# RWKV scan: whole transposes of the operands and of the inverse's levels, and direction 1 of A in the other half

## The reference

```python
def step(S, inp):
    rt, wt, kt, vt, at, bt = inp
    sa = jnp.einsum('bhvk,bhk->bhv', S, at)
    S = S * wt[:, :, None, :] + sa[..., None] * bt[:, :, None, :] + vt[..., None] * kt[:, :, None, :]
    return S, jnp.einsum('bhvk,bhk->bhv', S, rt)
```

## Time and profile before

| | |
|---|---|
| median of 3 runs | 2064.91 us (2064.57 to 2065.87) |
| profiled execution | 2068.68 us, span 2066.9 us |
| PE, PEld busy | 1737.8 us (84%), 1360.4 us (66%) |
| VectorE, ScalarE, GpSimd busy | 1111.6, 845.5, 288.4 us |
| the scan, 644 to 1113 us | PE 417.96 (x14716), PEld 403.63 (x14708), DVE 165.42, ACT 157.36, POOL 141.55 us busy |
| the stage ahead, 60 to 400 us | PE 340.00 us of 340 busy |
| mean granted TensorE clock | 0.929 of 2.4 GHz |

### The profile page before, as it was taken

The page is one execution under the profiler, slowest core; times in us unless marked ns, Lnnn a source line. Parts: engine busy times, 40 slices in busy tenths (PEclk is TensorE's granted clock), DMA queues, the critical chain, the costliest instruction groups (busy, mean ns, idle before and its releaser), DMA issues. The chain is left out here.

```text
span 2066.9 us, 47853 instructions
## 1 busy us (share of the span) xinstructions
PE 1737.8 (84%) x20423; PEld 1360.4 (66%) x20423; DVE 1111.6 (54%) x1786; ACT 845.5 (41%) x1228; POOL 288.4 (14%) x371
## 2 busy tenths in 40 slices
PE   5999999869896998989885698059999999999980
PEld 4777777757655888888885477046666666666650
DVE  4568898456753333333335632446565565656546
ACT  4256665212222333333332221046566565655632
POOL 0010000011103223332233000220000000000003
PEclk8999999989997999999997798579999999999995
DMA  5124454241102111111312121639998998999837
GB/s 170 62 93 136 137 147 123 66 158 62 61 1 91 49 55 55 55 30 54 145 65 84 54 73 50 247 132 378 362 381 348 372 371 350 377 363 379 350 143 254
DMA packets 95706, 355.62 MB, mean 172 GB/s; under 512 B 8984, under 2 KB 52295, under 8 KB 80936
## 3 DMA queue, kind: packets, MB, share of 16 engines
q1 hardware_dynamic: 82344, 306.83, 39.8%
q0 software_dynamic: 8576, 29.37, 3.7%
q10 hardware_dynamic: 4608, 16.78, 2.0%
HBM read 294.72 MB, written 56.13 MB: 170 GB/s over the span
## 5 line engine op out<-in xcount | busy, mean ns | idle before, releaser
L2236 DVE TENSOR_TENSOR e_rl<-proj,e_rh 128x1024 fp32r<-128x1024 f32 x256 | 304.9, 1222 | 150.1 <-ACT e_rh L2177 148.8
L2177 ACT ACTIVATE e_rh<-proj 128x1024 fp32r<-128x1024 f32 x256 | 258.6, 1053 | 82.4 <-PEq L1884 50.5
L51 PE MATMUL e_ph<-e_rh,e_xh 128*128 128x512 f32 x512 | 221.5, 433 | 17.1 <-DVE e_rl L2236 14.5
L2163 PE MATMUL e_py<-mix,proj 128*128 128x512 f32 x512 | 225.0, 592 | 0.7 <-issue 0.7
L51 PE MATMUL e_ph<-e_rh,e_xl 128*128 128x512 f32 x512 | 201.8, 394 | 0.0
L51 PE MATMUL e_ph<-e_rl,e_xh 128*128 128x512 f32 x512 | 200.5, 392 | 0.0
L51 PE MATMUL a_b<-a_xh,a_wh 128*128 128x512 f32 x432 | 177.9, 412 | 5.9 <-DVE a_wl L580 3.4
L51 PE MATMUL a_b<-a_xl,a_wh 128*128 128x512 f32 x432 | 170.2, 394 | 0.0
L51 PE MATMUL a_b<-a_xh,a_wl 128*128 128x512 f32 x432 | 170.2, 394 | 0.0
L2163 PEld LDWEIGHTS e_py<-mix,proj 128*128 128x128 f32 x512 | 97.1, 190 | 110.5 <-issue 108.1
L1544 ACT ACTIVATE s_th<-s_thb 128x512 f32<-128x512 f32 x128 | 76.4, 597 | 188.4 <-PE s_thb L1413 188.4
(11 more groups left out here) (352 smaller groups left out, 3260.1 us busy)
## 6 DMA issues: line engine op xcount, KB each, us to landing
proj<-in_moe_w SPq DMA_DIRECT2D x64, 2048.0 KB, 14.5
mix<-in_moe_w SPq DMA_DIRECT2D x32, 2048.0 KB, 8.7
proj<-scan_operands SPq DMA_DIRECT2D x64, 320.0 KB, 4.1
scan_operands<-late SPq DMA_DIRECT2D x64, 256.0 KB, 2.6
expert_rows<-e_yo ACTq DMA_DIRECT2D x32, 512.0 KB, 11.2
proj<-in_w_in SPq DMA_DIRECT2D x27, 512.0 KB, 4.1
proj<-in_x SPq DMA_DIRECT2D x16, 512.0 KB, 6.2
expert_rows<-proj SPq DMA_DIRECT2D x1, 7680.0 KB, 24.8
```

The lines of the kernel that those rows point to most:

```text
L51: m = e.matmul(out, lhs[a], rhs[b], start=first and n == 0, stop=last and n == 2)
L2163: m = e.matmul(py[h][:, :], at[:, k, :], w2[j][:, k, h * HALF:(h + 1) * HALF], start=(k == 0), stop=(k == KF - 1))
L2177: e.activation(rh[s % RING][:, :], piece(j, s), ACT.Copy).then_inc(high, 1)
L2236: e.tensor_tensor(rl[s % RING][:, :], piece(j, s), rh[s % RING][:, :].bitcast(F32), ALU.subtract).then_inc(low, 1)
```

## The change

`turn` no longer transposes quarter by quarter: eight whole 128 x 128 transposes for each g turn A, K, V and B. A whole transpose exchanges chunk and head halves together, and its result for direction 0 lies in one bank and for direction 1 in another; ScalarE copies the first, VectorE the second.

In the inverse, levels 2 to 5 no longer make both H and T by matmuls. Only T is made (at the last level H); a whole transpose of T, two for each g, gives H, and ScalarE copies it (`hu`) once VectorE has added the identity to the level's products. The products of levels 2 to 5 go to all four quarters: the half that the result is written to changes between chunk and unit. Results that come from different row halves of the array go to different banks of PSUM. Level 1 stays on the diagonal. The level's results of one g now share a pair of banks, so level 1 waits for VectorE's copy of the last inverse (`hf_kept`).

For direction 1, A is stored with its two chunks exchanged, by two DMAs in place of one (`a_out` counts 48 a unit instead of 32), so that `products` can write the B-A product into the other half; it has 20 matmuls for each g instead of 16. `a_k_v` and `inverse_applied` then also use all four quarters. A constant `eyes`, four identities, replaces the broadcast one in L1472.

The diff, without renamings of the same kind:

```diff
@@ -197,7 +197,13 @@
                         store(u, d, OP_R, ep2[d], r_out)
                     for d in range(2):
                         e.wait_ge(ra_done, 2 * u + d + 1)
-                        store(u, d, OP_A, ea2[d], a_out)
+                        if d == 0:
+                            store(u, d, OP_A, ea2[d], a_out)
+                        else:
+                            p, at = span(u)
+                            for c in range(2):
+                                e.dma_start(S.ops[p, d, at // P:at // P + 4, :, OP_A, (1 - c) * CH:(2 - c) * CH].rearrange("t p c -> p t c"),
+                                            ea2[d].rearrange("p (t k c) -> p t k c", k=2, c=CH)[:, :, c, :]).then_inc(a_out, 16)
                         e.wait_ge(b_done, 2 * u + d + 1)
                         store(u, d, OP_B, a2[d], b_out)
...
-        th, xx = sb("s_th", [P, GP, HU, 2, CH]), sb("s_xx", [P, GP, HU, CH])
+        tt, xx = sb("s_tt", [P, GP, HU, CH]), sb("s_xx", [P, GP, 2, 2, CH])
+        hu = sb("s_hu", [P, GP, 2, 2 * CH])
-        pu = sb("s_pu", [P, GP, HU, 2 * CH])
+        pu = sb("s_pu", [P, 2, HU, 2 * CH])
...
-        xb = [ps(f"s_x{k}", [P, HALF]) for k in range(GP)]
-        thb = [ps(f"s_thb{k}", [P, HALF]) for k in range(GP)]
-        w = [ps(f"s_w{k}", [P, HALF]) for k in range(4)]
-        xs = [t[:, 0:HU * CH].rearrange("p (u c) -> p u c", u=HU) for t in xb]
-        ths = [t.rearrange("p (u q c) -> p u q c", u=HU, q=2) for t in thb]
+        lv = [ps(f"s_lv{k}", [P, 2, HALF]) for k in range(GP)]
+        wb = [ps(f"s_w{k}", [P, 2, HALF]) for k in range(2)]
+        w = [wb[k][:, j, :] for k in range(2) for j in range(2)]
+        bank = [t.rearrange("p (q c) -> p q c", q=4) for t in (*(lv[k][:, j, :] for k in range(GP) for j in range(2)), *w)]
+        xs = [t[:, :, 0:2 * CH].rearrange("p b (q c) -> p b q c", q=2) for t in lv]
+        ts = [t[:, :, 2 * CH:4 * CH].rearrange("p b (q c) -> p b q c", q=2) for t in lv]
+        hus = [t[:, 0, 4 * CH:8 * CH].rearrange("p (q c) -> p q c", q=2) for t in lv]
-        trb = [t.rearrange("p (d s c) -> p d s c", d=2, s=4) for t in w[2:4]]
-        akvb = w[2].rearrange("p (u c) -> p u c", u=2 * HU)
+        trb = [t.rearrange("p (s c) -> p s c", s=4) for t in w[2:4]]
+        akvb = wb[1][:, :, 0:HU * CH].rearrange("p d (u c) -> p d u c", u=HU)
...
                         for u, (h, d) in enumerate(units):
-                            for c in hs:
-                                i = mm(pub[g][c, u, :], hf[c, g, u, :], rec[j][c, g, h, d, 0:2 * CH], start=True, stop=True)
-                        i.then_inc(pu_full, 1)
+                            for c in range(2):
+                                r = hs[c ^ d]
+                                i = mm(pub[d][hs[c], 2 * g + h, :], hf[r, g, u, :], rec[j][r, g, h, d, 0:2 * CH], start=True, stop=True)
+                            if g == GP - 1 and h == 1:
+                                i.then_inc(pu_full, 1)
 
                 def outputs_by_v(m):
 
...
-                    for d in range(2):
-                        for k, s in ((0, OP_B), (1, OP_K)):
-                            for h, c in quarters:
-                                i = mm(gb[h][hs[c], d, k, :], op[j][hs[h], g, d, s, hs[c]],
-                                       op[j][hs[h], g, d, OP_R:OP_A + 1, hs[c]], start=True, stop=True)
+                    for k, s in ((0, OP_B), (1, OP_K)):
+                        for h, c in quarters:
+                            mm(gb[h][hs[c], 0, k, :], op[j][hs[h], g, 0, s, hs[c]],
+                               op[j][hs[h], g, 0, OP_R:OP_A + 1, hs[c]], start=True, stop=True)
+
+                    ra = op[j][:, g, 1, OP_R:OP_A + 1, :].rearrange("p s (c t) -> p (s c) t", c=2)
+                    for h, c in quarters:
+                        mm(gb[h][hs[c], 1, 1, :], op[j][hs[h], g, 1, OP_K, hs[c]],
+                           ra[hs[h], 0:4:3, :] if c == 0 else ra[hs[h], 1:3, :], start=True, stop=True)
+                    for h, c in quarters:
+                        mm(gb[h][hs[c], 1, 0, 0:CH], op[j][hs[h], g, 1, OP_B, hs[c]], ra[hs[h], c, :], start=True, stop=True)
+                    for h, c in quarters:
+                        i = mm(gb[h][hs[1 - c], 1, 0, CH:2 * CH], op[j][hs[h], g, 1, OP_B, hs[c]], ra[hs[h], 3 - c, :],
+                               start=True, stop=True)
                     i.then_inc(g_full, 1)
 
                 def turn(f, g, back):
 
                     j = f % 2
                     if g == 1:
-                        e.wait_ge(tm_kept, f * 2 + 1)
+                        e.wait_ge(tm_kept, f * 4 + 2)
                     elif back is not None:
                         e.wait_ge(y_kept, back + 1)
                     for d in range(2):
                         for s in range(OP_A, N_OP):
-                            for h, c in quarters:
-                                i = mm(trb[h][hs[c], d, s - OP_A, :], op[j][hs[h], g, d, s, hs[c]], S.ident[hs[h], hs[h]],
-                                       start=True, stop=True)
+                            i = e.transpose(trb[d][:, s - OP_A, :], op[j][:, g, d, s, :], S.ident[:, :])
                     i.then_inc(turned, 1)
 
                 def a_k_v(f):
                     j = f % 2
-                    e.wait_ge(tm_kept, f * 2 + 2)
+                    e.wait_ge(tm_kept, f * 4 + 4)
                     e.wait_ge(g_kept, f * 2 + 2)
                     for g in range(GP):
-                        for u, (h, d) in enumerate(units):
-                            for c in hs:
-                                i = mm(akvb[c, g * HU + u, :], slot(j, g, h, d, S_KA)[c, :], slot(j, g, h, d, S_V)[c, :],
-                                       start=True, stop=True)
+                        for h, d in units:
+                            for c in range(2):
+                                i = mm(akvb[hs[c ^ d], d, 2 * g + h, :], slot(j, g, h, d, S_KA)[hs[c], :],
+                                       slot(j, g, h, d, S_V)[hs[c], :], start=True, stop=True)
                     i.then_inc(akv_full, 1)
 
...
                         fill[9] = lambda: a_k_v(front)
+                    pairs = [(q, p) for q in range(2) for p in range(2)]
                     e.wait_ge(t1_kept, n + 1)
                     for l in range(1, LEVELS):
                         first, last = l == 1, l == LEVELS - 1
@@ -1396,21 +1421,31 @@
                         for g in range(GP):
                             if not first:
                                 e.wait_ge(th_kept, n * 8 + (2 * (l - 2) + g + 1))
-                            for u in range(HU):
-                                for c in hs:
-                                    i = mm(xs[g][c, u, :], al[c, l - 1, g * HU + u, :],
-                                           t1[c, g * HU + u, :] if first else th[c, g, u, 0, :], start=True, stop=True)
+                            elif n:
+                                e.wait_ge(hf_kept, (n - 1) * 2 + (g + 1))
+                            for q, p in pairs:
+                                u = 2 * q + p
+                                for c in range(2):
+                                    to = xs[g][hs[c], p, q, :] if first else xs[g][hs[p], c, q, :]
+                                    i = mm(to, al[hs[c], l - 1, g * HU + u, :],
+                                           t1[hs[c], g * HU + u, :] if first else tt[hs[c], g, u, :], start=True, stop=True)
+                            if not first:
+                                for q in range(2):
+                                    i = e.transpose(hus[g][:, q, :], tt[:, g, 2 * q:2 * q + 2, :].rearrange("p u c -> p (u c)"),
+                                                    S.ident[:, :])
                             i.then_inc(x_full, 1)
                         fill[2 * l - 2]()
                         for g in range(GP):
                             e.wait_ge(x_kept, n * 10 + (2 * (l - 1) + g + 1))
-                            for u in range(HU):
-                                h0 = lambda c: h1[c, g * HU + u, :] if first else th[c, g, u, 1, :]
-                                if not last:
-                                    for c in hs:
-                                        mm(ths[g][c, u, 0, :], h0(c), xx[c, g, u, :], start=True, stop=True)
-                                for c in hs:
-                                    i = mm(ths[g][c, u, 1, :], xx[c, g, u, :], h0(c), start=True, stop=True)
+                            if not first:
+                                e.wait_ge(hu_kept, n * 8 + (2 * (l - 2) + g + 1))
+                            for q, p in pairs:
+                                u = 2 * q + p
+                                for c in range(2):
+                                    h0 = h1[hs[c], g * HU + u, :] if first else hu[hs[p], g, q, c * CH:(c + 1) * CH]
+                                    x0 = xx[hs[c], g, p, q, :] if first else xx[hs[p], g, c, q, :]
```

(89 more changed lines are left out.)

13 lines of the change are left out of this document (7 added, 6 removed).

## The result

The changed kernel takes 1994.81 us (median of 4 runs, 1994.29 to 1995.6), the kernel before, run beside it, 2064.74 us: a ratio of 0.9665, 95% interval 0.9649 to 0.9681, or 70 us less. The forecast was 1970, with a range to 2012. The profiled execution took 1995.2 us.

What follows compares the result with a forecast made beforehand. It took PE's work and instruction arrival (128 pairs each 3.75 us), the larger per level, as bound. 84 us for 14 steps, 4 for the first, 7 for last and tail: 95 saved, 1970 us, range 1942 to 2012.

Steps and rivals of the forecast that it cites:

- The bound: Scan: besides PE's work, instruction arrival over q8 limits the step, 128 pairs each 3.75 us, 29.3 ns a pair.
- the prediction's sign against the fetch bound: Scan's q8 queue: intervals between instruction packets well below 3.5 us would disprove that instruction arrival limits PE.
- The saving is 28.0 - 22.0 = 6.0 us a step: Full scan step: sum over five levels of the larger of work and instruction fetch, before less after.
- the work of the changed step: Scan step after the change: PE's work alone, summed over five levels, 20.6 us.
- Two transposes between products: Inverse, levels 2 to 5: a pair of whole transposes with its switches costs PE 0.46 us.
- the first step: Scan's first step, without back work: 4 us saved of its 22.9.
- the last step with the tail: End of the scan: loses the same products without the turning, 7 us saved.
- Work alone (1950): Rival, scan: fetch is no bound, PE's work of 20.6 us sets the step, 20 us better; 13 in 100.
- The exposed stalls (2004): Rival, scan levels: two evictions in a row between products delay PE, about 0.6 us at four levels, 34 us; 19 in 100.
- The order of quarters: Rival, second products: two from one row half, then two from the other, run at 29 ns, 25 us, 1995; 7 in 100.
- The clock: Rival, scan: PE falls to 1.2 GHz, passes take twice the time, 256 us more, 2226; 8 in 100.
- The stage ahead: Stage before the scan: eight more store issues at 0.36 us, priced at zero; 2.9 us if cover is absent.

Runs made afterwards that it cites:

- batch: Changed kernel, but in levels 2 to 5 the products of both g come first, then the four whole transposes together; 1993.0 us, ratio 0.9656.
- turn_quarters: Changed kernel with the operands again turned quarter by quarter instead of by eight whole transposes; 2030.5 us, ratio 0.9817.
- turn_only: Kernel before with only the whole transposes of the operands, copied by ScalarE and VectorE side by side; 2031.1 us, ratio 0.9825.
- levels_only: Kernel before with only the new inverse levels, turned operands copied by ScalarE and VectorE side by side, A not exchanged; 2026.3 us, ratio 0.9798.
- no_swap: Changed kernel without the exchange of A's chunks in direction 1, its store one DMA again; 1991.9 us, ratio 0.9655.
- by_quarters: Changed kernel with outputs_by_v and outputs_by_u on all four quarters, same instruction count, scan outputs wrong; 1994.7 us, ratio 0.9655.
- best: Changed kernel without the exchange of A's chunks and with the clearing transfer moved into the next stage; 1983.3 us, ratio 0.9594.
- best_batch: Changed kernel without A's exchange, clearing transfer in the next stage, products of both g ahead of a level's four whole transposes; 1976.5 us, ratio 0.9565.
- all by ScalarE: Changed kernel with all turned operands copied by ScalarE, one after the other, instead of by ScalarE and VectorE; 1991.5 us, ratio 0.9632.

## Why the prediction was right, and where its sum was off

**The bound.** Right, where PE's work leaves room for it. Put the kernels in order of the pairs in a step, with the mean of the 15 intervals between their marks: 928 pairs, 28.9 us (before); 832, 26.5 (turned in quarters); 816, 26.3 and 26.0 (each part alone); 720, 24.2, 24.0 and 24.0 (changed, by quarters, batch); 704, 23.8 (no exchange). One line runs through them, 4.7 us for 208 pairs, 22.6 ns a pair. Each mean is of one execution, up to 5.4 us off its kernel's median, so 0.4 us between two of them mean nothing. At 720 pairs, work cut by 0.9 or 1.2 us moves the step by 0.2 to 0.3. There, what PE computes hardly matters; how many instructions it takes does. At 816 pairs with the old levels, and at 704, PE's work nearly fills the step, and both count.

The change itself cannot tell the two: it took work and pairs together, and PE's idle time ended by "issue" is 23 us of 284 before and 26 after (666 to 950 us). Only the runs that move one of the two do. That the gaps are waits for q8 can be read from the packets in the traces. In the kernels before, changed, `turn_quarters`, `turn_only`, `levels_only`, `no_swap`, `by_quarters`, `batch`, `best` and `best_batch`, every issue gap of PE over 0.3 us from 666 to 950 us ends 2.2 to 3.0 us after a packet's start (once 3.3), while the packets start 3.9 to 4.3 us apart on average and never under 3.2. So the prediction's sign against the fetch bound, intervals well below 3.5 us, did not come.

**The term that was off** is the size of the step's saving: "The saving is 28.0 - 22.0 = 6.0 us a step". Taking the larger of work and fetch level by level let a pair removed save 28.8 ns; it saved 22.6, and 208 of them 4.7 us. Two terms of it measured wrong. First the work of the changed step: one with a single stall for instructions, of about 0.84 us, takes 22.51 us (833.57 to 856.08), so 21.7 against 20.6. Two transposes between products cost 0.51 us and not 0.46, as the second starts 0.17 us after the first and not 0.109 (block 1.51 us against 1.41), and each `products` 1.15 us against 0.91, as its first group after the transposes takes 0.71 us for 16 passes (844.99 to 845.70). Second, and larger: 24.07 against the 21.7 of work are 2.4 us of gaps a step. Arrival at one packet in 3.75 us gives 720 pairs in 21.1 us; measured is a packet in 24.07/5.63 = 4.3 us, and before 28.7/7.25 = 4.0. The pace is not fixed. One thing that the sum left out shows in the packets: where the scan's own operand loads move over 200 KB between two packet starts, these are 4.9 us apart before and 5.1 after; where they move nearly nothing, 3.7 and 3.9. These loads have the same size in every step however short the step is, so they weigh more in a short one. Beyond that, a fast group seems not to draw on the time of a slow one as freely as my sum assumed. What keeps instructions from arriving further ahead is open; no run varied it, nor the loads. That the total came within 25 us owes a little to luck: the first step gained 2.0 us more than forecast and the last step with the tail 2.3 less, and the two cancel.

**Work alone (1950)** is refuted by the gaps and the turning in quarters. **The exposed stalls (2004)** came nearest in time, 9 us off, but not as told: the round of evictions can be moved (batch, all by ScalarE) without effect, and L1591's and L1597's copies last 0.38 us as priced. PE waits for ScalarE's `hu` only 0.6 us in all of 651 to 950 us. **The order of quarters** did nothing: L1448's 32 passes (products two by two from one row half, then from the other) let the next group start after 0.47 us, 14.7 ns each, like the rest. The Trainium skill, "TensorE: Matmul & The Clock Gate", section "Part 3: Packing small matmuls — row/col tiling", has weight loads overlap matmuls in flight only where the row groups differ; by it this rival's 29 ns should have come, and these rows show 14.7. **The clock** stayed at its upper level (0.99 over 651 to 950 us) with 16 + 16 whole transposes a step; in the step under the clearing it fell for a while, to 0.84 on average between 952 and 985 us, where PE was busy 25.0 of 33 us. The price of this rival was too high: it set 1.93 us, the length of 64 turning passes at the lower level, against 0.98, the distance between two starts at the upper. The length at the upper level is 1.16, so the factor of these rows is 1.7 and not 2.

**The other terms.** Turning: 0.96 us for eight transposes (853.69 to 854.65), priced at 1.12. A-k-v 0.52 against 0.49. The stage ahead, with its eight stores more: the scan's first mark comes 0.8 us later (644.5 against 643.7), but over all runs it lies between 640.2 and 646.7, and the latest has no such stores; so a cost of them is not shown, and 0 stands. First step 6.0 us against 4, last step and tail 4.7 against 7, contended step 3.9 against 6.

## What to carry to other kernels

Where matmuls are so small that PE takes 15 to 30 ns each, count its instructions and look at the queue that brings them: if PE's idle time has no cause in the profile and always ends soon after one of that queue's packets, fewer instructions help and faster ones do not, and a bulk transfer on the same DMA engines costs PE time although it shares no data. A whole transpose by one matmul in place of eight quarter passes is worth its switches there; where work bounds it should be worth nothing, as eight transposes and 64 passes cost PE the same (0.96 and 1 us). Test such a bound with two kernels, one that changes the work at equal instructions and one that changes the instructions at equal work.

## What the runs showed of the hardware that was not expected

- Marginal price of a weight-load and matmul pair in this scan: 22.6 ns over the kernels from 928 to 704 pairs, where a whole transpose of 128 x 128 counts as one pair like a quarter pass.
- PE's gaps without a visible cause end 2.2 to 3.0 us after the start of a packet of q8, in ten kernels. A packet brings 128 pairs, and two start at least 3.2 us apart; 4.9 to 5.1 us where operand loads run, 6.0 to 7.3 us under the clearing transfer.
- A 7.7 MB transfer beside such a stage cost it 8 to 11 us; in the next stage it cost 1.3 us at most.
- The second of two whole transposes after a change from quarters starts 0.17 us after the first (0.44 less 0.27, the modelled length of one); in a run of eight the mean distance is 0.11 ((1.04 - 0.27)/7).
- PE fell to the lower clock for a part of the step in which its instructions came late: 0.84 on average over 33 us in the changed kernel, 0.95 over 37.5 us before.
